# Mixer column blocks multiplied with tokens on partitions and moved through DRAM, and one half-to-half product per SSD group

## The chip, the cores and the metric

One core of one Trainium2 chip. The metric is the device time of the whole kernel in microseconds, the median of repeated runs.

## The reference

One layer of a hybrid block on 256 tokens of width 2048, all float32: a half-step SwiGLU FFN, a mixer, and a second FFN, each behind an RMS norm with adaLN modulation from a vector c. What matters here is the mixer:

```python
u = hn @ w_in                      # 2048 columns -> z, xbc, dt, q, k, v, q_idx, k_idx, w_idx, gates
xbc = silu(causal_dwconv(xbc, conv_w, conv_b))    # 4 taps along the tokens; xs, B and C
# SSD scan, per group of 4 heads (8 groups, state 128, head size 64)
y_diag = einsum('btsg,btsgr,bsgrp->btgrp', cb, decay, xc)
y_off  = einsum('btgn,bgrpn,btgr->btgrp', cc, state, exp(acum))
y = rms((y + d_skip * xs) * silu(z)) per group
y_att = top-k sparse attention(q, k, v, q_idx, k_idx, w_idx)
merged = g0 * (y_ssd @ w_br_ssd) + g1 * (y_att @ w_br_att);  out = merged @ w_out
```

## The kernel before

Every weight is used in units of 256 rows by 512 columns (512 KB). SP loads a unit into one of four slots of `raw` (L733). ScalarE rounds it to `w_hi` (L1002, `cast`), VectorE takes the rest, `w_lo` = `raw` - `w_hi` (L1536, `sub`), and TensorE multiplies it in three terms. There are four slots of `w_hi` and `w_lo`: the cast of unit n waits until unit n-4 is multiplied, and the load of unit n until unit n-4 is subtracted. So ScalarE and VectorE can be up to three units ahead of TensorE. There are 850 units in all.

The order of everything else is written out by hand. Each engine runs one loop over the unit number n; at fixed distances from a block's start or end it does the side work of that n after its own cast or subtraction (on TensorE before the unit). An engine works strictly in its order, so a wait in side work holds back the casts, subtractions or units behind it.

The mixer multiplies `w_in` in 20 column blocks of 8 units (`WBLOCKS`): b 0 and 1, c 2 and 3, xs 4 to 7, z 8 to 11, index queries qi 12 and 13, k 14, v 15, q 16 to 19. Two units of narrow front columns (step sizes, index key and weights) lie between blocks 1 and 2. Block b goes to PSUM banks 2 (b % 2) and the next; block b+2 waits for `pair_read[b % 2]`.

- Blocks of kind z, k, v, q use `unit` (L2433): tokens on partitions, 128 tokens stationary, 512 weight columns moving, 12 matmuls a unit.
- Blocks 1 to 7, 12 and 13 use `fm_unit` (L2733): 128 weight columns stationary, 256 tokens moving, 24 matmuls a unit, so that channels lie on partitions. The convolution and the index products need that layout.

After a b, c or xs block ScalarE copies the product from PSUM (`conv_in`, L1234, at n = end + 2) into `padded` and, scaled and biased, into `conv`; VectorE adds three taps, four instructions each, at end + 3, 4, 5 (`conv_tap`, L2042); ScalarE applies SiLU at end + 6. xs blocks must go back to tokens on partitions: VectorE turns them in 32x32 blocks at end + 7 (`xs_bands`, L2056), POOL stores them to DRAM, waits, and reads them back in four DMAs (L941, L910), and ScalarE spreads them at end + 13 (`xs_out`, L1275). The same trip serves the FFN activations (L1803, L916, L919, L1113) and others.

The SSD work runs by group g from `ssd_start[g]` (s): TensorE makes the B-C products at s (L2794); VectorE the segments at s + 2 (L2113); ScalarE the exponentials at s + 3: `decay_off`, four instructions for the half-to-half decay (L1364), and one for the other two; VectorE the masked decays at s + 4 (three products, `ssd_mask`, L2142); TensorE twelve products at s + 5 (`ssd_y`, L2803); VectorE the gating at s + 7 (L2153 to L2158) and the normalisation and turning at s + 9. Step sizes (`dt_first`, `dt_rest`, L2076 to L2103) are worked out at 5 and 7 to 10 units after the front columns, the cumulative sums (L2783) at block 4. The index products are one every two units from block 14 on, the top-k rounds (L2236) in the first q block, 16.

Between all this VectorE keeps adding up adaLN vectors (L1556, `ada_add`) on the units that `light` picks. Weight rows for it are loaded by SP (L739), 512 KB each.

The diff touches, beside declarations: `light`, the SP loop, the POOL loop of the mixer, `conv_in`, `qi_out`, `decay_off`, `decay_exp` and the ScalarE mixer loop, `conv_tap`, `cum_out`, `ssd_mask`, `ssd_gate` and the VectorE mixer loop, `fm_unit`, `ssd_products`, `ssd_y`, `index` and the TensorE mixer loop.

Of the kernel before, what the change touches and what calls it, by code (L numbers as in the profile page):

```python
# [23 lines left out]
F32 = mybir.dt.float32  # L24
# [6 lines left out]
P = 128  # L31
T = 256
# [88 lines left out]
def build(nc, x, c, positions, w_ada, b_ada, norm_ffn1, ffn1_w1, ffn1_w3, ffn1_w2, norm_mix, w_in,  # L121
# [50 lines left out]
    xs_raw = place("xs_raw", at_h + 4 * KB, [BANDS, UNIT // BANDS])  # L172
    kiT = place("kiT", region(T * 4), [T])
# [8 lines left out]
    acum = place("acum", region(3 * SSD_H * 4), [3, SSD_H])  # L182
# [50 lines left out]
    decay = place("decay", at_y, [3, 4, P])  # L233
    cb = place("cb", at_y + 6 * KB, [3, P])
# [36 lines left out]
    xs_dram = nc.dram_tensor("xs_bands", (P, BANDS, UNIT // BANDS), F32).ap()  # L271
    y_dram = nc.dram_tensor("y_bands", (P, BANDS, P), F32).ap()
# [79 lines left out]
    conv_out = sem("conv_out")  # L352
    xs_blocked = sem("xs_blocked")
# [19 lines left out]
    off_ready = sem("off_ready")  # L373
# [67 lines left out]
    ssd_start = [start[at_block["z"] + 1 + g] for g in range(GROUPS)]  # L441
# [286 lines left out]
    def _(sp):  # L728
# [18 lines left out]
        for f in range(2):  # L747
# [90 lines left out]
    def _(pool):  # L838
# [97 lines left out]
        for n in range(MIX, M1):  # L936
            for b in range(NW):
                if kind[b] == "xs" and n == end[b] + 7:
# [31 lines left out]
    def _(act):  # L970
# [263 lines left out]
        def conv_in(b):  # L1234

            act.wait_ge(unit_done, end[b])
# [74 lines left out]
        def qi_out(b):  # L1311
            i = WBLOCKS[b][1]
            act.wait_ge(unit_done, end[b])
            for j in range(2):
                ins = nc.scalar.activation(qiT[:, 4 * i + 2 * j:4 * i + 2 * j + 2, :],
                                           psum[:, pair(b) + j, :].rearrange("p (k t) -> p k t", k=2), ACT.Copy)
            ins.then_inc(pair_read[b % 2], 1)
# [46 lines left out]
        def decay_off(g):  # L1364
# [1688 lines left out]
```

## Time and profile before

| | |
|---|---|
| median of 3 runs | 2501.76 us (2498.63 to 2503.24) |
| profiled execution | 2502.94 us, span 2501.2 us |
| granted TensorE clock | 0.999 of full speed over the span |
| TensorE, VectorE, ScalarE, POOL busy | 99%, 75%, 47%, 7% |
| DRAM traffic | 642.76 MB, mean 257 GB/s |

The profile times single instructions of the profiled execution, in microseconds from the start of the span. The difference between span and time (1.74) lies outside the span. A matmul's duration overlaps with that of the next, so lengths of TensorE work are read from starts to starts. An idle time has behind it what ended it.

### The profile page before, as it was taken

The page shows a single profiled execution, that of the slowest core. Times are in us where ns is not written, and L with a number is a line of the kernel's source. Part 1 is how long each engine was busy: PE and PEld are TensorE (multiplying, and loading weights), DVE is VectorE, ACT ScalarE, POOL GpSimd, SP SyncE. Part 2 cuts the span into 40 slices and gives each one's busy share as a digit, 9 for nine tenths or more (in the row PEclk, how much of TensorE's full clock was granted, in tenths as well). Part 3 has the DMA queues.
Part 4 walks back from the last instruction along what each step waited for, and adds up shares of the span by engine and source line. Part 5 has one row for each costly group of instructions (what it writes and reads, how often), then busy time and mean ns, then how long its engine had stood idle before and what let it go on. Part 6 is the DMA issues. An engine that isn't in the chain of part 4 may idle for free.

```text
span 2501.2 us, 33094 instructions
## 1 busy us (share of the span) xinstructions
PE 2467.9 (99%) x12067; PEld 2080.9 (83%) x12067; DVE 1871.6 (75%) x2124; ACT 1167.4 (47%) x1431; POOL 169.9 (7%) x273
## 2 busy tenths in 40 slices
PE   7999999999999999999999999999999999999999
PEld 5788888888889999898788888888788888888887
DVE  6886679898988989988975677776789555555556
ACT  4444444444446655655555444444544444444443
POOL 4210000000000000111100000000000000000000
PEclk9999999999999999999999999999999999999999
DMA  9986679999986889985544788796698767677775
GB/s 366 376 285 191 192 246 364 311 359 304 360 289 222 274 279 317 317 251 177 177 139 139 255 278 292 255 316 242 224 318 299 224 210 210 209 210 208 211 210 173
DMA packets 290611, 642.76 MB, mean 257 GB/s; under 512 B 26066, under 2 KB 26676, under 8 KB 289588
## 3 DMA queue, kind: packets, MB, share of 16 engines
q1 hardware_dynamic: 269600, 571.41, 69.5%
q0 software_dynamic: 19136, 65.05, 7.9%
q10 hardware_dynamic: 1748, 4.62, 0.5%
q8 instruction: 78, 1.28, 0.2%
q14 instruction: 49, 0.40, 0.0%
HBM read 622.59 MB, written 18.41 MB: 256 GB/s over the span
## 4 chain that ended last, share of the span: by engine, by line
PE 91%; DVE 5%; DMA 2%; issue 1%; ACT 1%; ACTq 0%; DVEq 0%; SPq 0%
PE psum L2443 26%; PE psum L2445 26%; PE psum L2444 26%; PE psum L2743 3%; PE psum L2745 3%; PE psum L2744 3%; PE psum L2781 2%; DMA raw<-in_ffn_w 1%; DVE w_lo L1536 1%; PE psum L2431 1%; DVE ada_acc L1650 1%; DMA badas<-in_b_ada 0%; DMA gate_mix<-gate_rows 0%; PE psum L2524 0%; ACT w_hi L1002 0%
## 5 line engine op out<-in xcount | busy, mean ns | idle before, releaser
L1536 DVE TENSOR_TENSOR w_lo<-raw,w_hi 128x1024 fp32r<-128x1024 f32 (+1 forms) x850 | 1032.9, 1220 | 477.6 <-ACT w_hi L1002 475.7
L1002 ACT ACTIVATE w_hi<-raw 128x1024 fp32r<-128x1024 f32 (+1 forms) x850 | 898.2, 1059 | 1041.1 <-PE psum L2445 801.6
L2443 PE MATMUL psum<-w_hi,xT_hi 128*128 128x512 f32 x1984 | 782.3, 394 | 5.4 <-issue 3.5
L2445 PE MATMUL psum<-w_hi,xT_lo 128*128 128x512 f32 x1984 | 773.3, 390 | 0.0
L2444 PE MATMUL psum<-w_lo,xT_hi 128*128 128x512 f32 x1984 | 772.8, 390 | 0.0
L2443 PEld LDWEIGHTS psum<-w_hi,xT_hi 128*128 128x128 f32 x1984 | 372.9, 188 | 88.4 <-issue 8.7
L2445 PEld LDWEIGHTS psum<-w_hi,xT_lo 128*128 128x128 f32 x1984 | 372.7, 188 | 78.7
L2444 PEld LDWEIGHTS psum<-w_lo,xT_hi 128*128 128x128 f32 x1984 | 373.0, 188 | 76.1
L2443 PE MATMUL psum<-w_hi,aT_hi 128*128 128x512 f32 x704 | 274.8, 390 | 2.3 <-DVE aT_lo L1811 2.3
L2445 PE MATMUL psum<-w_hi,aT_lo 128*128 128x512 f32 x704 | 274.0, 389 | 0.0
L2444 PE MATMUL psum<-w_lo,aT_hi 128*128 128x512 f32 x704 | 273.9, 389 | 0.0
L1556 DVE SCALAR_TENSOR_TENSOR ada_acc<-ada_raw,cact,ada_acc 128x1024 f32<-128x1024 f32 x210 | 268.3, 1278 | 2.7 <-DMA ada_raw<-in_w_ada 2.7
L2743 PE MATMUL psum<-xT_hi,w_hi 128*128 128x256 f32 x576 | 163.6, 284 | 1.1 <-DVE w_lo L1536 1.1
L2745 PE MATMUL psum<-xT_hi,w_lo 128*128 128x256 f32 x576 | 163.0, 283 | 0.0
L2744 PE MATMUL psum<-xT_lo,w_hi 128*128 128x256 f32 x576 | 163.0, 283 | 0.0
L2443 PEld LDWEIGHTS psum<-w_hi,aT_hi 128*128 128x128 f32 x704 | 132.1, 188 | 30.5 <-issue 3.1
L2445 PEld LDWEIGHTS psum<-w_hi,aT_lo 128*128 128x128 f32 x704 | 132.1, 188 | 27.6
L2444 PEld LDWEIGHTS psum<-w_lo,aT_hi 128*128 128x128 f32 x704 | 132.2, 188 | 27.2
L1828 DVE TENSOR_TENSOR y<-psum,y 128x1024 f32<-128x1024 f32 x89 | 108.7, 1221 | 21.2 <-PE psum L2445 21.2
L2743 PEld LDWEIGHTS psum<-xT_hi,w_hi 128*128 128x128 f32 x576 | 110.5, 192 | 1.2 <-issue 1.2
L2744 PEld LDWEIGHTS psum<-xT_lo,w_hi 128*128 128x128 f32 x576 | 110.5, 192 | 0.0
L2745 PEld LDWEIGHTS psum<-xT_hi,w_lo 128*128 128x128 f32 x576 | 110.5, 192 | 0.0
(285 smaller groups left out, 2069.8 us busy)
## 6 DMA issues: line engine op xcount, KB each, us to landing
raw<-in_ffn_w SPq DMA_DIRECT2D x528, 512.0 KB, 4.6
ada_raw<-in_w_ada SPq DMA_DIRECT2D x224, 512.0 KB, 6.3
raw<-in_w_in SPq DMA_DIRECT2D x224, 512.0 KB, 4.6
ada_raw<-in_w_ada POOLq DMA_DIRECT2D x32, 512.0 KB, 6.9
ada_more<-in_w_ada POOLq DMA_DIRECT2D x32, 512.0 KB, 7.7
raw<-in_w_br_ssd SPq DMA_DIRECT2D x32, 512.0 KB, 5.3
raw<-in_w_br_att SPq DMA_DIRECT2D x32, 512.0 KB, 4.7
raw<-in_w_out SPq DMA_DIRECT2D x32, 512.0 KB, 5.2
```

The lines of the kernel that those rows point to most:

```text
L1002: nc.scalar.activation(w_hi[:, n.slot(SPLIT), 0:size], raw[:, n.slot(RAW), 0:size], ACT.Copy).then_inc(hi_ready, 1)
L1536: nc.vector.tensor_tensor(w_lo[:, n.slot(SPLIT), 0:size], raw[:, n.slot(RAW), 0:size], w_hi[:, n.slot(SPLIT), 0:size], ALU.subtract).then_ ...
L1556: nc.vector.scalar_tensor_tensor(out=acc[:], in0=src, scalar=cact[:, k:k + 1], in1=acc[:], op0=ALU.mult, op1=ALU.add).then_inc(ada_used, 1)
L1650: ins = nc.vector.scalar_tensor_tensor(out=acc[:, cols], in0=row[:, cols], scalar=cact[:, k + r:k + r + 1], in1=acc[:, cols], op0=ALU.mult ...
L1828: nc.vector.tensor_tensor(y[:, :, cols], psum[:, bank:bank + HALF, :], y[:, :, cols], ALU.add).then_inc(y_added, 1)
L2443: nc.tensor.matmul(o, hi[:, kt + k, toks], whi, start=a, stop=False)
L2444: nc.tensor.matmul(o, hi[:, kt + k, toks], wlo, start=False, stop=False)
L2445: ins = nc.tensor.matmul(o, lo[:, kt + k, toks], whi, start=False, stop=b)
L2743: nc.tensor.matmul(o, w_hi[:, s, cols], xT_hi[:, kt + k, :], start=a, stop=False, skip_group_check=True)
L2744: nc.tensor.matmul(o, w_hi[:, s, cols], xT_lo[:, kt + k, :], start=False, stop=False, skip_group_check=True)
L2745: ins = nc.tensor.matmul(o, w_lo[:, s, cols], xT_hi[:, kt + k, :], start=False, stop=b, skip_group_check=True)
L2781: return nc.tensor.matmul(o, a, b, start=first, stop=last)
```

## The change

Blocks 1 to 7, 12 and 13 are multiplied with `unit` as the others, and `fm_unit` is gone. At end + 2 VectorE turns the product from PSUM in 32x32 blocks into `mix_blk` (two instructions of 512 columns, new `product_bands`); POOL stores it to DRAM (512 KB), waits for the store, and reads it back in four DMAs of 128 KB into `mix_raw`. ScalarE reads that at end + 8 (`READ_AT`), in `conv_in` or `qi_out`, instead of PSUM at end + 2. The taps follow at +1, +2, +3, SiLU at +4, the turning of xs at +5 and `xs_out` at +11 from there; block 0 keeps its places. `ssd_start` moves four units later for every group, and `light` keeps adaLN adds off other units. There is one `mix_blk` and one `mix_raw`.

Per group, the half-to-half part no longer has a decay matrix: the decay is split into a factor per source token (with the step size, `acum[:, 2]`) and one per target token (`acum[:, 3]`), exponentiated once for all groups (`far_decay`, `far_weights`). VectorE scales xs by the first (`x_far`), TensorE multiplies once with the B-C product, 256 columns, into bank 4, and VectorE scales the result by the second (`y_far`) and adds it.

The core of the diff:

```diff
+    BANDED = [b for b in range(1, NW) if kind[b] in ("b", "c", "xs", "qi")]
+    READ_AT = 8
+    conv_at = [end[b] + (READ_AT if b else 2) for b in range(at_block["z"])]
-    ssd_start = [start[at_block["z"] + 1 + g] for g in range(GROUPS)]
+    ssd_start = [start[at_block["z"] + 1 + g] + UPB // 2 for g in range(GROUPS)]
...
-        return w % UPB not in (3, 4, 5) if w < 9 * UPB else w == 9 * UPB + 1 or w % UPB in (0, 3, 5, 6)
+        return w % UPB not in (1, 2, 3) if w < 10 * UPB else w % UPB in (1, 2, 4, 7)
...
                         if g >= 2:
-                            sp.wait_ge(off_ready, g - 1)
...
+                if b in BANDED and n == end[b] + 2:
+                    i = BANDED.index(b)
+                    pool.wait_ge(pair_read[b % 2], b // 2 + 1)
+                    if i:
+                        pool.wait_ge(mix_read, i)
+                    pool.dma_start(mix_dram, mix_blk[:]).then_inc(mix_stored, 16)
+                    pool.wait_ge(mix_stored, 16 * (i + 1))
+                    bands_to(mix_raw, mix_dram, mix_moved)
...
+                act.wait_ge(mix_moved, 16 * BANDS * (BANDED.index(b) + 1))
...
-            for j in range(2):
-                src = psum[:, pair(b) + j, :].rearrange("p (k t) -> p k t", k=2)
-                nc.scalar.activation(padded[:, b % 2, 2 * j:2 * j + 2, 3:3 + T], src, ACT.Copy)
+            for half in range(HALF):
+                dst = padded[:, b % 2, :, 3 + half * P:3 + (half + 1) * P].rearrange("p k (b t) -> p k b t", t=32)
+                nc.scalar.activation(dst, by_bands(half, mix_raw), ACT.Copy)
...
-                ins = nc.scalar.activation(conv[:, k, :], psum[:, pair(b) + k // 2, (k % 2) * T:(k % 2 + 1) * T],
+                ins = nc.scalar.activation(y_tokens(conv, k), mix_bands(k),
...
-            ins.then_inc(pair_read[b % 2], 1)
+            ins.then_inc(mix_read, 1)
...
-            for k in range(4):
-                ins = nc.scalar.activation(decay[:, 1, k, :], cum_spread[:, g % 2, k, P:T], ACT.Exp,
-                                           bias=acum[:, 2, 4 * g + k:4 * g + k + 1])
-            ins.then_inc(off_ready, 1)
+        def far_decay():
+
             act.wait_ge(acum_ready, 1)
+            nc.scalar.activation(acum[:, 2:4, :], acum[:, 2:4, :], ACT.Exp).then_inc(far_exp, 1)
...
                 if n == CUM_AT + 2:
                     cum_copy()
+                    far_decay()
...
+        def product_bands(b):
+
+            i = BANDED.index(b)
+            dve.wait_ge(unit_done, end[b])
+            dve.wait_ge(h_spilled, 16)
+            if i:
+                dve.wait_ge(mix_stored, 16 * i)
+            for half in range(HALF):
+                ins = nc.vector.transpose(mix_blk[:].rearrange("p c (k s t) -> p s k c t", s=HALF, t=32)[:, half],
+                                          psum[:, pair(b) + half, :].rearrange("p (k c t) -> p k c t", c=BANDS, t=32))
+            ins.then_inc(pair_read[b % 2], 1)
...
+            dve.wait_ge(far_ready, 1)
+            nc.vector.tensor_tensor(x_far[:], heads4(xs[:, g])[:, 0], head_cols(2, g), ALU.mult)
-            for j in range(3):
+            for j in (0, 2):
...
+            nc.vector.tensor_tensor(y_far[:], psum[:, 4, 0:T].rearrange("p (k d) -> p k d", k=4), head_cols(3, g),
+                                    ALU.mult).then_inc(y_step, 1)
...
+            nc.vector.tensor_tensor(yg2[:, 1, :], yg2[:, 1, :], y_far[:].rearrange("p k d -> p (k d)"), ALU.add).then_inc(y_step, 1)
...
+                pe.wait_ge(y_step, 4 * g - 2)
...
-                o = psum[:, 7, T + k * 64:T + (k + 1) * 64]
-                plain(o, decay[:, 1, k, :], xdt[:, 0, k, :], True, False)
-                ins = plain(o, decay[:, 2, k, :], xdt[:, 1, k, :], False, True)
-            ins.then_inc(y_raw, 1)
+                plain(psum[:, 7, T + k * 64:T + (k + 1) * 64], decay[:, 2, k, :], xdt[:, 1, k, :])
+            plain(psum[:, 4, 0:T], cb[:, 1, :], x_far[:].rearrange("p k d -> p (k d)")).then_inc(y_raw, 1)
...
-                if kind[b] in ("b", "c", "xs", "qi"):
-                    fm_unit(n, 2 * u, 2 * (b % 2), u == 0, u == UPB - 1)
-                else:
-                    unit(At(n), xT_hi, xT_lo, 2 * u, 2 * (b % 2), u == 0, u == UPB - 1)
+                unit(At(n), xT_hi, xT_lo, 2 * u, 2 * (b % 2), u == 0, u == UPB - 1)
```

## Rows read from the trace of the kernel before

**Rows 1.** The page: busy time, and the chain that ended last.
```profile
PE 2467.9 (99%) x12067; PEld 2080.9 (83%) x12067; DVE 1871.6 (75%) x2124; ACT 1167.4 (47%) x1431; POOL 169.9 (7%) x273
...
PE 91%; DVE 5%; DMA 2%; issue 1%; ACT 1%; ACTq 0%; DVEq 0%; SPq 0%
```

**Rows 2.** The chain in order of time: start, length, what.
```profile
887.21 1.26 PE psum L2781 x10
...
980.70 0.23 PE psum L2443
...
1002.49 0.65 PE psum L2781 x4
...
1016.77 2.62 PE psum L2781 x24
...
1242.64 0.86 PE psum L2781 x4
```

**Rows 3.** ScalarE's timeline at block 6: start, length, line, what, idle before.
```profile
934.66 1.09 ACT L1257 ACTIVATE padded<-psum 128x512 f32<-128x512 f32 x2 [1.76 <-PE psum L2745]
...
937.42 2.03 ACT L1002 ACTIVATE w_hi<-raw 128x1024 fp32r<-128x1024 f32 x2
```

**Rows 4.** VectorE's timeline at the same place.
```profile
938.54 1.22 DVE L1536 TENSOR_TENSOR w_lo<-raw,w_hi 128x1024 fp32r<-128x1024 f32 x1 [2.12 <-ACT w_hi L1002]
939.68 1.67 DVE L2052 SCALAR_TENSOR_TENSOR conv<-padded,convT,conv 128x256 f32<-128x256 f32 x4
941.27 1.22 DVE L1536 TENSOR_TENSOR w_lo<-raw,w_hi 128x1024 fp32r<-128x1024 f32 x1
```

**Rows 5.** Busy time by stretch: the top-k rounds.
```profile
1188.00:1230.00 42.00, 40.27 (x193) 32.84 (x191) 41.45 (x105) 21.34 (x32) 9.53 (x14) 1.00 0.53 152
```

**Rows 6.** Timelines of VectorE, POOL and ScalarE: three trips through DRAM.
```profile
951.53 1.30 DVE L2064 STREAM_TRANSPOSE xs_blk<-conv 128x512 f32<-128x512 f32 x2
953.13 0.56 POOL L941 DMA_DIRECT2D xs_bands<-xs_blk  x1 [16.92 <-DVE xs_blk L2064]
958.12 2.18 POOL L910 DMA_DIRECT2D xs_raw<-xs_bands  x4 [4.43 <-DMA xs_bands<-xs_blk]
968.10 1.34 ACT L1283 ACTIVATE xs<-xs_raw 128x256 f32<-128x256 f32 x4 [3.52 <-DMA xs_raw<-xs_bands]
...
975.10 1.30 DVE L2064 STREAM_TRANSPOSE xs_blk<-conv 128x512 f32<-128x512 f32 x2
...
992.43 1.34 ACT L1283 ACTIVATE xs<-xs_raw 128x256 f32<-128x256 f32 x4 [5.10 <-DMA xs_raw<-xs_bands]
...
1842.93 1.31 DVE L1803 STREAM_TRANSPOSE act_blk<-act_tok 128x512 f32<-128x512 f32 x2
...
1857.96 1.15 ACT L1113 ACTIVATE aT_hi<-aT_raw 128x512 fp32r<-128x512 f32 x2 [2.33 <-DMA aT_raw<-act_bands]
```

**Rows 7.** ScalarE's timeline at the front columns.
```profile
853.43 0.20 ACT L1301 ACTIVATE wi<-psum 128x32 f32<-128x32 f32 x1 [0.79 <-DVE sp_e L2080]
...
853.99 1.28 ACT L1305 ACT_TABLE_LOAD   x1
...
855.45 1.99 ACT L1002 ACTIVATE w_hi<-raw 128x1024 fp32r<-128x1024 f32 x2
```

**Rows 8.** VectorE's timeline at the step-size series.
```profile
857.66 1.28 DVE L1556 SCALAR_TENSOR_TENSOR ada_acc<-ada_raw,cact,ada_acc 128x1024 f32<-128x1024 f32 x1
858.86 0.19 DVE L2087 TENSOR_SCALAR sp_s<-sp_e 128x64 f32<-128x64 f32 x1
...
860.41 1.23 DVE L1536 TENSOR_TENSOR w_lo<-raw,w_hi 128x1024 fp32r<-128x1024 f32 x1
...
862.75 0.74 DVE L2093 SCALAR_TENSOR_TENSOR sp_p<-sp_p,sp_e 128x64 f32<-128x64 f32 x3
```

**Rows 9.** Busy time of block 7 (last two columns: DMA share, GB/s); DMA traffic of 10 to 60 us.
```profile
957.00:980.70 23.70, 23.70 (x199) 23.70 (x198) 21.32 (x28) 13.23 (x19) 2.74 (x5) 1.00 1.00 337
...
DMA packets 6778, 18.92 MB, mean 378 GB/s; under 512 B 665, under 2 KB 993, under 8 KB 6777
```

More of the change, by code:

```diff
@@ L937, in _ @@
             for b in range(NW):
-                if kind[b] == "xs" and n == end[b] + 7:
+                if b in BANDED and n == end[b] + 2:
[6 more added lines that the diff above has]
+                    bands_to(mix_raw, mix_dram, mix_moved)
+                if kind[b] == "xs" and n == conv_at[b] + 5:
                     i = WBLOCKS[b][1]
@@ L1234, in conv_in @@
         def conv_in(b):
-            act.wait_ge(unit_done, end[b])
+            if b == 0:
+                act.wait_ge(unit_done, end[b])
+            else:
+                act.wait_ge(mix_moved, 16 * BANDS * (BANDED.index(b) + 1))
             act.wait_ge(pads, 1)
@@ L1312, in qi_out @@
             i = WBLOCKS[b][1]
[L1313 to L1317, printed above, removed]
+            act.wait_ge(mix_moved, 16 * BANDS * (BANDED.index(b) + 1))
+            for half in range(HALF):
+                ins = nc.scalar.activation(by_tokens(qiT[:, 4 * i:4 * i + 4, :], half), by_bands(half, mix_raw), ACT.Copy)
+            ins.then_inc(mix_read, 1)
         def v_out(b):
@@ L1440, in mixer @@
                     if kind[b] in ("b", "c", "xs"):
-                        if n == end[b] + 2:
+                        if n == conv_at[b]:
                             conv_in(b)
-                        if n == end[b] + 6:
+                        if n == conv_at[b] + 4:
                             conv_silu(b)
-                        if kind[b] == "xs" and n == end[b] + 13:
+                        if kind[b] == "xs" and n == conv_at[b] + 11:
                             xs_out(b)
+                    if kind[b] == "qi" and n == end[b] + READ_AT:
+                        qi_out(b)
                     if n == end[b] + 2:
@@ L2044, in conv_tap @@
             if j == 0:
-                dve.wait_ge(pair_read[b % 2], b // 2 + 1)
+                dve.wait_ge(mix_read, BANDED.index(b) + 1) if b else dve.wait_ge(pair_read[0], 1)
                 dve.wait_ge(pads, 1)
@@ L2054, in conv_tap @@
                                                op0=ALU.mult, op1=ALU.add).then_inc(taps, 1)
+        def product_bands(b):
[4 more added lines that the diff above has]
+                dve.wait_ge(mix_stored, 16 * i)
+            for half in range(HALF):
+                ins = nc.vector.transpose(mix_blk[:].rearrange("p c (k s t) -> p s k c t", s=HALF, t=32)[:, half],
+                                          psum[:, pair(b) + half, :].rearrange("p (k c t) -> p k c t", c=BANDS, t=32))
+            ins.then_inc(pair_read[b % 2], 1)
         def xs_bands(b):
@@ L2324, in mixer @@
                 for b in range(NW):
-                    if kind[b] in ("b", "c", "xs") and n in (end[b] + 3, end[b] + 4, end[b] + 5):
-                        conv_tap(b, n - end[b] - 3)
-                    if kind[b] == "xs" and n == end[b] + 7:
+                    if b in BANDED and n == end[b] + 2:
+                        product_bands(b)
+                for b in range(NW):
+                    if kind[b] in ("b", "c", "xs") and n - conv_at[b] in (1, 2, 3):
+                        conv_tap(b, n - conv_at[b] - 1)
+                    if kind[b] == "xs" and n == conv_at[b] + 5:
                         xs_bands(b)
@@ L2731, in ffn @@
                         turn_gate((2, 8)[f], GATE_BANK[2 * f])
-        def fm_unit(n, kt, bank, first, last):
-            pe.wait_ge(split_ready, n + 1)
-            s = n % SPLIT
-            for j in range(4):
-                o = psum[:, bank + j // 2, (j % 2) * T:(j % 2 + 1) * T]
-                for k in range(2):
-                    cols = slice(k * NB + j * P, k * NB + (j + 1) * P)
-                    a, b = first and k == 0 and j % 2 == 0, last and k == 1
-                    nc.tensor.matmul(o, w_hi[:, s, cols], xT_hi[:, kt + k, :], start=a, stop=False, skip_group_check=True)
-                    nc.tensor.matmul(o, w_hi[:, s, cols], xT_lo[:, kt + k, :], start=False, stop=False, skip_group_check=True)
-                    ins = nc.tensor.matmul(o, w_lo[:, s, cols], xT_hi[:, kt + k, :], start=False, stop=b, skip_group_check=True)
-            ins.then_inc(unit_done, 1)
         def plain_unit(n, kt, first, last):
```

41 lines of the change are left out of this document (26 added, 15 removed).

## The prediction

> **What bounds the kernel now.** I read the page first: TensorE is busy 99% of the span and carries 91% of the chain that ended last [rows 1]. So a shorter TensorE stream is worth its own length wherever VectorE, ScalarE and the DMAs keep up, and the question is the mixer, where VectorE is 9 tenths busy. Then I read the chain in order of time [rows 2]. From 888.47 (887.21 and the 1.26 of the cumulative sums) to 980.70 run four column blocks in the old form, 23.06 us each, or 2.88 us a unit of 24 matmuls. From 980.70 to 1002.49 runs a block in the form that the change spreads to all: 21.79 us, 2.72 us a unit of 12 matmuls. The twelve products of a group take 2.62 us. Both stretches have no hole: TensorE bounds them.
>
> **What hides the rest today** is a lead. ScalarE may cast a unit once the unit four places ahead of it is done, so VectorE runs up to three units ahead of TensorE. I read the VectorE and ScalarE timelines for what consumes that lead. Today the copy of a finished block waits only for TensorE: it starts at 934.66, the next cast at 937.42 [rows 3], the next subtraction at 938.54 [rows 4]. Everything in the sum below is made of such steps.
>
> **The change part by part.**
>
> *Matmuls.* Nine blocks of eight units, each unit 2.88 to 2.72: 0.16 x 72 = 11.3 us less TensorE work. In block 1 (the second "b" block) VectorE already sets the pace, so only some 0.4 of its 1.3 can show.
>
> *Group products.* Twelve products at 2.62/12 = 0.22 become eight (1.75) and one of 256 columns; two such take 0.86 [rows 2], so 0.43. 2.62 to 2.18, 0.44 x 8 = 3.5 us less.
>
> *The removed exponentials* (four on ScalarE per group) are not on the path, since ScalarE is half idle (busy 47% [rows 1]): nothing. *VectorE per group:* one decay product less, two 256-wide and one PSUM product more: about +0.4 us beside 24.7 us of TensorE work: nothing either. *The last-but-one stretch*, from 1188, where VectorE has the top-k rounds and works 41.45 of 42 us [rows 5]: groups move four units later, so one gate and one normalisation leave the rounds and land behind them. I add the same durations up both ways and get TensorE about 0.7 us earlier. *SP:* no DMA more; one wait less. *POOL:* per block one store, a wait and four reads, 0.56 + 2.18 us of issuing [rows 6], in a queue that is otherwise waiting.
>
> *The round trip.* This decides. The product of a block is turned at unit 2 after its end, and is read by ScalarE at unit 8. Rows of the same trip (512 KB out, four reads of 128 KB, same queue) give the time from the first transpose to ScalarE's start when ScalarE sat waiting for it: 951.53 to 968.10 = 16.6, 975.10 to 992.43 = 17.3, 1842.93 to 1857.96 = 15.0 [rows 6]. The trace doesn't show this trip beside a second one. I take the mean, 16.3, for blocks 1 to 4 and the largest, 17.3, for blocks 5 to 7, where the old xs trip shares the DMA queues; the ends for the range are 15.0, and 19 as an estimate (17.3 and a tenth more, for the larger traffic).
>
> *The loop.* ScalarE can't cast unit 1 of the next block until it has read the trip (2.76 [rows 3]; strided reads from SBUF, I take the same). VectorE then subtracts, runs four taps, subtracts, and only then turns the next block: 1.14 + 1.59 + 1.14 = 3.9 [rows 4]. So from one turning to the next: trip 16.3 + copy 2.8 + cast 1.1 + 3.9 = 24.1 us, against 21.8 us of TensorE. No lead survives a loop that is 2.3 us too long per block. Today it doesn't exist: the copy hangs on TensorE alone.
>
> Step by step, time 0 being the end of block 1, and "ready" the end of a unit's subtraction, which is 16.3 + 5.0 after a turning:
> - Trip 1 starts at 0.3. ScalarE reads it at unit 6 of block 2, and there also does the front columns, 853.43 to 855.45 = 2.0 [rows 7]. Unit 7 is ready at 23.6; TensorE wants it at 24.9 (5.8 for two front units, seven of 2.72).
> - Now the taps of block 1 fall on the units in which the step-size series is worked out (1.55, then 0.7 to 1.1 [rows 8]) and an adaLN add (1.2 [rows 8]) is kept. The next four units are ready 5.5, 4.7, 3.5 and 3.5 later: 40.8 for unit 3 of block 3, wanted at 35.8. Stall 5.0.
> - Trip 2 (37.3) makes unit 1 of block 4 ready at 58.6; TensorE is there at 58.4.
> - In block 4 the new exponential of the far weights waits on ScalarE for VectorE's unit 2, which now holds turning, taps and copies (1.2 + 1.6 + 0.5), then loads a table (1.28 [rows 7]) and exponentiates (0.3); the cast of unit 3 is queued behind, and its subtraction: 68.4 instead of 64.0. Stall 4.4, and 0.6 for the table that goes back. Trip 3 (61.3) hides in it.
> - Trip 4 (86.5): unit 1 of block 6 at 107.8. Trips 5, 6, 7, with 17.3, are loops of 25.0: 132.8, 157.8, 182.8.
>
> Before, the same stretch (to unit 1 of block 9) is 5.8 + 6 x 23.06 + 21.8 + 2.7 + 1.3 + 0.2 for two small transposes = 170.2. So this stretch gets **12.6 us longer**, though its TensorE work is 7.6 us shorter.
>
> Behind it the DMAs are lighter, the groups' TensorE work grows to 24.7 per block, and the lead comes back; the two index blocks turn their products with no taps behind: 2 x 1.3 gained, 3.5 from the groups, 0.7 from the top-k stretch, and 0.7 lost in block 9, which starts with no lead.
>
> Sum: +12.6 - 0.4 - 2.6 - 3.5 - 0.7 + 0.7 = **+6.1 us**. The profiled execution took 2502.94 (span 2501.2), 1.2 above the median of 2501.76. Against the median the forecast is 2508, slower by 0.25%; 0.2% (5 us) is about what a measurement of this kernel can tell from no change.
>
> *DMA traffic.* A block with the old xs trip moves 8.0 MB today (23.7 us at 337 GB/s, share 1.00), and one with both trips 9.0: over the 25.0 us of the loop 360 GB/s. The trace has held 378 GB/s for 50 us [rows 9], so I give it no stall of its own. The Trainium skill (DMA: Bandwidth & Descriptors, Specifications) puts the limit of HBM at about 358 GB/s for a core. By that rule 9.0 MB would need an estimated 25.1 us, which leaves the sum with the loop where it is and would take some 8 us from a version without it; the trace, at 378, disagrees.
>
> **The rivals.**
> 1. *The lead holds, and the kernel is faster.* If the trips are short enough, the loop fits under a block of TensorE work and every stall but those of blocks 3 and 4 goes. For it: today an xs trip blocks ScalarE for up to 5.1 us per block and TensorE never stops. Against it: that trip is followed by a copy which hangs on TensorE, so its lateness isn't handed on. It decides from a trip of 14.0 us down (21.8 - 2.8 - 1.1 - 3.9), shorter than any row shows. Worth -11.3 - 3.5 - 0.7 with 0.9 lost in block 1, about 2 in the clashes of blocks 3 and 4, 1 elsewhere: -11.6, 2490.
> 2. *Short trips.* The loop as I say but all trips at 15.0: 1.3 less for the first trip, 1.3 + 3 x 2.3 for the last four: -9.5 on my sum, -3.4, so 2498.
> 3. *The DMAs bind.* The raw loads and the two trips share one set of queues, and casts wait for weights. At the 337 GB/s of today's fullest block [rows 9] 9.0 MB take 26.7 us, 1.7 more than my loop in blocks 6 and 7 and half of that in block 8, and the longer xs trip then delays unit 4 as well, about 1 in each: +7.3 on the sum, 2515. It decides from about 360 GB/s down, the rate that my loop itself asks for.
> 4. *The new form isn't shorter here.* It stands in the same stage at 2.72 a unit [rows 2], so this has almost no chance.
>
> **How the numbers follow.** My case 0.47 (its own range 2502 to 2513; about two thirds of its chance lie above 2506.8), rival 1 0.18, rival 2 0.18, rival 3 0.15, rival 4 0.02. Slower by over 0.2% (above 2506.8): 0.31 + 0.15 = 0.46. Faster by over 0.2% (below 2496.8): 0.18 and a quarter of rival 2, together 0.22. Within: what is left, 0.32. The range reaches from just above rival 1 to just above rival 3: 2491 to 2516.
>
> **What would show it.** In the changed profile: units of the nine blocks at 2.72 and group products at 2.18; TensorE idle until VectorE's subtraction in blocks 3 to 8, 15 to 20 us in all, and nearly none before; ScalarE waiting for the trip in each of them and VectorE for ScalarE's cast; turnings 24 to 25 us apart; one idle of some 4 us in block 4, behind the far exponential. I am wrong if the turnings are 21.8 apart with TensorE solid (rival 1), or if casts wait for weights rather than for the trip (rival 3).

## The result: 2520.3 us, slower by 0.75%

The changed kernel took 2520.3 us in the median of 4 runs (2516.1 to 2522.6), the kernel before 2501.75 (2498.6 to 2503.2) beside it: ratio 1.0075, 95% interval 1.0063 to 1.0087. I forecast 2508 and a range to 2516. The sign was right, the size was a third of what came.

The profile after, first the page's lines that answer to [rows 1]:

```profile
span 2520.9 us, 31318 instructions
PE 2466.6 (98%) x11155; PEld 2034.4 (81%) x11155; DVE 1886.5 (75%) x2160; ACT 1161.0 (46%) x1402; POOL 194.8 (8%) x318
...
PE 82%; DVE 7%; DMA 6%; ACT 2%; issue 2%; POOL 0%; ACTq 0%; DVEq 0%; SPq 0%
```

TensorE has the shorter stream, and its share of the chain fell from 91% to 82%; the DMAs' rose from 2% to 6%. The chain in order of time shows one turn of what took its place (start, length, what):

```profile
871.87 1.32 DVE mix_blk L2082 x2
...
873.47 5.03 DMA mix_bands<-mix_blk
...
878.78 1.63 POOL mix_raw L925 x3
880.41 8.59 DMA mix_raw<-mix_bands
...
890.09 2.06 ACT conv L1286 x4
892.15 0.96 ACT w_hi L1025
...
894.27 1.66 DVE conv L2070 x4
895.94 1.14 DVE w_lo L1554
897.07 1.23 DVE mix_blk L2082 x2
```

From turning to turning, no TensorE in it: VectorE turns, the bands go to DRAM and come back, ScalarE reads them and only then casts, VectorE subtracts, runs taps, subtracts and turns the next block. I call this chain, which ends where it begins, the ring. ScalarE's timeline has the waits for the trips, at the end of each:

```profile
850.99 1.16 ACT L1283 ACTIVATE padded<-mix_raw 128x512 f32<-128x512 f32 x2 [4.28 <-DMA mix_raw<-mix_bands]
889.03 1.15 ACT L1283 ACTIVATE padded<-mix_raw 128x512 f32<-128x512 f32 x2 [2.97 <-DMA mix_raw<-mix_bands]
912.93 1.16 ACT L1283 ACTIVATE padded<-mix_raw 128x512 f32<-128x512 f32 x2 [0.30 <-DMA mix_raw<-mix_bands]
938.84 1.16 ACT L1283 ACTIVATE padded<-mix_raw 128x512 f32<-128x512 f32 x2
964.78 1.16 ACT L1283 ACTIVATE padded<-mix_raw 128x512 f32<-128x512 f32 x2 [4.81 <-DMA mix_raw<-mix_bands]
991.43 1.16 ACT L1283 ACTIVATE padded<-mix_raw 128x512 f32<-128x512 f32 x2 [3.73 <-DMA mix_raw<-mix_bands]
1018.53 1.16 ACT L1283 ACTIVATE padded<-mix_raw 128x512 f32<-128x512 f32 x2 [3.72 <-DMA mix_raw<-mix_bands]
```

VectorE in turn waits for ScalarE's cast, and TensorE for VectorE's subtraction. The two engines behind the reading at 964.78:

```profile
968.89 1.22 DVE L1554 TENSOR_TENSOR w_lo<-raw,w_hi 128x1024 fp32r<-128x1024 f32 x1 [3.65 <-ACT w_hi L1025]
970.03 1.67 DVE L2070 SCALAR_TENSOR_TENSOR conv<-padded,convT,conv 128x256 f32<-128x256 f32 x4
971.61 1.22 DVE L1554 TENSOR_TENSOR w_lo<-raw,w_hi 128x1024 fp32r<-128x1024 f32 x1
972.75 1.30 DVE L2082 STREAM_TRANSPOSE mix_blk<-psum 128x512 f32<-128x512 f32 x2
...
970.16 0.50 PE L2494 MATMUL psum<-w_hi,xT_hi 128*128 128x512 f32 x1 [2.25 <-DVE w_lo L1554]
```

The turnings (VectorE, L2082) stand at 833.46, 871.87, 896.99, 920.91, 946.81, 972.75 and 999.39. So from the second on the trips take 17.2, 15.9, 17.9, 18.0, 18.7 and 19.1, the turnings come 25.1, 23.9, 25.9, 25.9 and 26.6 apart, and each period is its trip and 8.0 us. Between 800 and 1300 us TensorE shows 18 idles of over 0.5 us, some 30 us together (before: 3, 3.1 us). Idles are counted here and below from start to start, less the usual distance of two matmuls; the timeline's own idle times are up to 0.2 us shorter.

A reading that I had not looked for stands behind the longer idles. Granted clock (after the busy times of PE, PEld, DVE, ACT, POOL) in two windows of ten microseconds:

```profile
core 0: us, PE busy (x) PEld busy (x) DVE busy (x) ACT busy (x) POOL busy (x), PEclk, DMA share, GB/s
900.00:910.00 10.00, 7.33 (x25) 5.78 (x25) 8.71 (x13) 7.45 (x8) 2.18 (x4) 0.83 0.84 256
1020.00:1030.00 10.00, 7.26 (x20) 5.43 (x19) 7.37 (x13) 7.74 (x14) 2.18 (x4) 0.66 0.82 254
```

In the second, TensorE idles for 2.9 us from 1021.0, and the next 13 matmuls stand 0.43 us apart instead of 0.23: the lower of its two levels, 1.2 GHz for 2.4. Between 800 and 1300 us three such stretches follow idles (8, 13 and 7 matmuls, 5.6 us more than at full clock); in the kernel before there is none there.

**Where the time went**, by TensorE's timeline. Up to the end of block 1 the two executions differ by 3.4 us in favour of the changed kernel, of which at most 0.4 can be its units in block 1: the rest is the same program, and executions of one kernel vary by as much. From there to unit 1 of block 9 the kernel before took 834.92 to 1005.73, 170.8 us; the changed one 831.56 to 1023.91, 192.3: 21.5 us more. The next 13 matmuls run at half clock, 2.6 more. Up to the last index product (block 15) 6.6 come back, behind it 5.4 go: 2.2 of these are only the products of one group, which now stand behind that point instead of ahead of it, and 3.2 are lost, where the top-k rounds are. Together 22.9, less 3.4: the 19.5 by which the spans differ (19.7). The medians differ by 18.6.

### The profile page after: what moved, and what is told of

Read it like the earlier page. It is cut to its first block, busy times and chain, and to the rows that moved or that the text cites. A ratio compares the mean times of both kernels' runs of the same rounds, so it can differ in the third digit from the quotient of the medians.

```text
span 2520.9 us, 31318 instructions
## 1 busy us (share of the span) xinstructions
PE 2466.6 (98%) x11155; PEld 2034.4 (81%) x11155; DVE 1886.5 (75%) x2160; ACT 1161.0 (46%) x1402; POOL 194.8 (8%) x318
## 4 chain that ended last, share of the span: by engine, by line
PE 82%; DVE 7%; DMA 6%; ACT 2%; issue 2%; POOL 0%; ACTq 0%; DVEq 0%; SPq 0%
PE psum L2494 26%; PE psum L2496 26%; PE psum L2495 26%; DVE w_lo L1554 2%; PE psum L2817 2%; DMA mix_raw<-mix_bands 2%; DMA raw<-in_ffn_w 2%; DMA mix_bands<-mix_blk 1%; PE psum L2482 1%; DVE conv L2070 1%; ACT w_hi L1025 1%; DVE ada_acc L1668 1%; ACT conv L1286 0%; POOL mix_raw L925 0%; DVE mix_blk L2082 0%
## 5 line engine op out<-in xcount | busy, mean ns | idle before, releaser
L2494 PE MATMUL psum<-w_hi,xT_hi 128*128 128x512 f32 x2272 | 900.8, 396 | 32.1 <-DVE w_lo L1554 29.2
L2495 PE MATMUL psum<-w_lo,xT_hi 128*128 128x512 f32 x2272 | 888.4, 391 | 0.0
L2496 PE MATMUL psum<-w_hi,xT_lo 128*128 128x512 f32 x2272 | 888.0, 391 | 0.0
L2494 PEld LDWEIGHTS psum<-w_hi,xT_hi 128*128 128x128 f32 x2272 | 428.7, 189 | 136.2 <-DVE w_lo L1554 32.1
L2496 PEld LDWEIGHTS psum<-w_hi,xT_lo 128*128 128x128 f32 x2272 | 428.6, 189 | 91.0
L2495 PEld LDWEIGHTS psum<-w_lo,xT_hi 128*128 128x128 f32 x2272 | 428.7, 189 | 87.0
L2494 PE MATMUL psum<-w_hi,yT_hi 128*128 128x512 f32 x128 | 50.6, 395 | 0.0
L2494 PE MATMUL psum<-w_hi,mT_hi 128*128 128x512 f32 x128 | 50.5, 395 | 0.0
L2496 PE MATMUL psum<-w_hi,mT_lo 128*128 128x512 f32 x128 | 50.0, 390 | 0.0
L2496 PE MATMUL psum<-w_hi,yT_lo 128*128 128x512 f32 x128 | 49.9, 390 | 0.0
```

Source lines behind the costliest of these rows:

```text
L2494: nc.tensor.matmul(o, hi[:, kt + k, toks], whi, start=a, stop=False)
L2495: nc.tensor.matmul(o, hi[:, kt + k, toks], wlo, start=False, stop=False)
L2496: ins = nc.tensor.matmul(o, lo[:, kt + k, toks], whi, start=False, stop=b)
```

## The experiments

All ratios are to the kernel before on the same chip, with their 95% intervals.

**1. The ring opened: the reading later.**

```
 READ_AT = 8
+CONV_READ = 10
-conv_at = [end[b] + (READ_AT if b else 2) ...]
+conv_at = [end[b] + (CONV_READ if b else 2) ...]
-return w % UPB not in (1, 2, 3) if w < 10 * UPB ...
+return w % UPB not in (3, 4, 5) if w < 10 * UPB ...
...
```

The second edit moves the adaLN adds off the units that now hold the taps. The first SSD group also waits for the last taps and the last turning of xs, which come later.

> The changed kernel with one schedule number moved: ScalarE reads the mixer trips of the tap blocks at unit 10 after a block's end instead of 8, so the taps, the cumulative-sum copies excepted, come two units later, and ScalarE's reading no longer stands ahead of the cast that VectorE needs before the next turning. Loop theory (trip, then copy, cast, four taps and the next turning in a ring): the ring is open, turnings come 21.8 to 22.9 us apart in blocks 4 to 9, about 15 us of TensorE's 21 lost in blocks 3 to 9 come back, together with the stretches at half clock: about 2505 us (2500 to 2511), ratio to before 1.001. The old xs trip has a ring of its own (trip 16.6, copy 2.9, cast 1.1, two subtractions 2.3 = 22.9), which may keep some 3 us of that. Rival, the DMAs bind: the same bytes in the same blocks, so turnings stay 25 to 26 us apart and the time at 2517 to 2522.

Measured: 2506.2 us, ratio 1.0029 (1.0020 to 1.0039), 11.5 us less than the changed kernel by the two ratios. ScalarE never waits for the mixer trip any more. The ring was the largest part of the loss, as the first theory said. Its size was not as I had said. The 2505 looks met, but the kernel before took 2499.7 beside this run, so the ratio is 1.0029 and not 1.001: 11.5 us came back, not 15. The turnings are 24.7, 22.2, 24.0, 23.1 and 25.9 apart, not 21.8 to 22.9, and TensorE keeps 11 idles of over 0.5 us, 17.0 us together. That is for experiments 6 to 8.

Here, too, three of the five periods are turning to reading plus a fixed rest, 2.5 us, which is VectorE's subtraction and add between a cast and the turning. So a fixed rest alone doesn't show a ring. What does are the waits for the trip, which are gone here, and the time that their end gives back.

**2. Fewer bytes beside the ring, and fewer bytes in it.** The first leaves out the xs trip, 1 MB for each of four blocks:

```
-act.wait_ge(xs_moved, 16 * BANDS * (i + 1))
+act.wait_ge(xs_blocked, i + 1)
...
-src = xs_raw[:] ...
+src = xs_blk[:] ...
...
-pool.dma_start(xs_dram, xs_blk[:]).then_inc(xs_stored, 16)
-pool.wait_ge(xs_stored, 16 * (i + 1))
-bands_to(xs_raw, xs_dram, xs_moved)
...
```

> The changed kernel without the old xs trip through DRAM (ScalarE copies from the transposed tile in SBUF, so the xs values stand in the wrong order): 1 MB less for each of four blocks, and ScalarE never waits for it. The mixer ring is untouched. Theory that the traffic of the second trip lengthens the first one: the trips of blocks 5 to 8 fall from 17.9-19.1 to about 16.3 us, the turnings from 25.9-26.7 to about 24.1 apart, total about 2512 us. Rival, a trip takes its 18 us whatever runs beside it: turnings stay above 25.5 apart, total 2517 to 2520.

Measured: 1.0075 (1.0061 to 1.0089), no change at all; turnings 24.2, 22.7, 26.5, 25.3 and 26.1 apart, the last three trips 17.3, 18.1 and 17.6 long (18.0, 18.7 and 19.1 in the changed kernel). My theory that the second trip lengthens the first by some 2 us fell. The last three are 0.6 to 1.5 us shorter here, but trips at the same place differ from trace to trace, too: in experiment 4, where no byte is left out, the same three took 17.9, 17.9 and 18.6. So little of a trip can be the xs trip's doing. The second has the mixer trips carry half of their bytes:

```
-pool.dma_start(mix_dram, mix_blk[:]).then_inc(mix_stored, 16)
+pool.dma_start(mix_dram[0:64], mix_blk[0:64]).then_inc(mix_stored, 16)
...
-bands_to(mix_raw, mix_dram, mix_moved)
+for to in range(BANDS):
+    pool.dma_start(mix_raw[32 * to:32 * (to + 1), 0:2], mix_dram[0:64, to, :]...)
...
```

> The changed kernel, the mixer trips with half of their bytes: two of the four token bands go to DRAM (256 KB) and come back (four reads of 64 KB), the rest of the tile is zero, so half of each turned product is missing; waits, queues and the number of instructions stay. The bytes taken away (0.5 MB written and 0.5 MB read for a block) are as many as dropping the xs trip takes, which moved neither the time nor the turnings. Ring theory: trips of 12 to 14 us, the ring of 20 to 22 us fits under TensorE's 21.8, turnings 22 to 23 apart from block 4 on: about 2509 us (2506 to 2512). Rival, the bytes on the shared queues matter and not where they are in the ring: as without the xs trip, 2518.

Measured: 1.0022 (1.0013 to 1.0031), 13 us less than the changed kernel. The turning of block 3, ScalarE's reading of it and the next turning, from its two timelines:

```profile
917.26 1.30 DVE L2088 STREAM_TRANSPOSE mix_blk<-psum 128x512 f32<-128x512 f32 x2
...
933.60 1.16 ACT L1289 ACTIVATE padded<-mix_raw 128x512 f32<-128x512 f32 x2 [1.85 <-DMA mix_raw<-mix_bands]
...
941.57 1.31 DVE L2088 STREAM_TRANSPOSE mix_blk<-psum 128x512 f32<-128x512 f32 x2
```

Trip 16.3, period 24.3, difference 8.0. Over its five periods the trips are 14.8, 13.9, 16.3, 15.3 and 15.6, the periods 22.7, 22.2, 24.3, 23.2 and 23.6: again trip + 8.0 in each (8.2 once). In two of the five (13.9 and 15.6) ScalarE came from a cast that had waited for its weights and no longer for the trip, so there the trip is no longer what sets the period. The trips shrank less than I said (12 to 14), since half of the bytes is not half of the time.

The two runs take about the same out of the DRAM traffic of the whole kernel, 4.2 MB without the xs trip and 4.7 MB here. (For one block the expectation counts double: the half trip saves 0.25 MB written and 0.25 MB read, against 0.5 and 0.5 for the xs trip.) At the one place none of the loss comes back, at the other 13 us: the trip's place in the ring is shown.

**3. Is VectorE's load the brake of the changed kernel?** In the adaLN adds of blocks 4 to 9 only 4 columns are added:

```
+few = 32 <= mixed[0] - FRONT_END + 2 * UPB < 80
-ada_add(At(e * KT + k), k)
+ada_add(At(e * KT + k), k, slice(0, 4) if few else slice(0, ADA_COLS))
```

> The changed kernel, the adaLN adds of blocks 4 to 9 on 4 columns instead of 1024 (so most of these sums is left out; their loads stay). VectorE does some 27 adds of 1.2 us less there. Ring theory: no add stands in the ring (trip, copy, cast, subtraction, taps, subtraction, turning), so the turnings stay trip + 8.0 us apart, 25 to 26.5, and the time at 2516 to 2520. Rival, VectorE's load (22.5 us of work in a block of an xs column) is what stops TensorE: turnings 22 to 23 apart, about 2506.

Measured: 1.0082 (1.0068 to 1.0096), periods 24.8, 23.0, 26.0, 25.3 and 26.9 with trips of 16.8, 15.0, 18.0, 17.3 and 18.9: trip + 8.0 once more. VectorE works 22 us less (22 adds shortened by 1 us each, not the 27 that I had counted on), and it gives nothing, because none of it stands in the ring.

**4. The far exponential in block 4.**

```
 if n == CUM_AT + 2:
     cum_copy()
-    far_decay()
+if n == CUM_AT + 6:
+    far_decay()
...
-if n == CUM_AT + 3:
+if n == CUM_AT + 7:
     far_weights()
```

> The changed kernel with the far weights' exponential (and VectorE's product behind it) four units later. In the trace it costs 2.8 us of idle and a stretch at half clock in block 4. By the steps of my prediction that stall hid the ring's own, and taking it away gives 2.7 us: 2517.5. By the ring as measured (trip 17 + 8.0 = 25 from the turning at 897.1, the next one stands at 921.0 already) nothing is left to give back: 2519 to 2521. Rival, the whole of idle and half clock comes back: 4 us, 2516.

Measured: 2518.2 us, 1.0073 (1.0059 to 1.0087). The difference to the changed kernel, 0.5 us, lies inside both intervals, and between the three numbers that I had written down this one can't choose with certainty; it is nearest to the ring's (0). The periods in the trace do: 25.0 and 23.8 around block 4, against 25.1 and 23.9 with the exponential in its place. The same move in the kernel of experiment 1:

> The kernel with the late reading, and the exponential of the far weights four units later in block 4. In the changed kernel it stood in front of a cast and cost a 2.8 us idle and a stretch at half clock; with the late reading block 4 shows no idle above 0.5 us, since the taps no longer share its unit. Expected: nothing, 2505 to 2507. Rival, it still delays a cast and the lead: 2 us less, 2504.

Measured: 1.0027 (1.0016 to 1.0038) against 1.0029: nothing, as expected.

**5. The group part alone, and its start four units later.** To the kernel before, first only the far weights, the one product per group and VectorE's two added operations, with `ssd_start` and the places of the adds as they were:

> The kernel before with the group part of the change alone (one half-to-half product per group, far weights, two more VectorE operations), at its old place, no block turned. By my sum: 0.44 us of TensorE less in each of eight groups, no stall: about 2498 us, ratio 0.9986. Rival, the far exponential and VectorE's extra work eat it: 2501 to 2503.

Measured: 2498.3 us, 0.9990 (0.9981 to 0.9999), 2.5 us less; I had 3.5. Then with the changed kernel's start and its places for the adaLN adds:

```
-ssd_start = [start[at_block["z"] + 1 + g] for g in range(GROUPS)]
+ssd_start = [start[at_block["z"] + 1 + g] + UPB // 2 for g in range(GROUPS)]
...
-return w % UPB not in (3, 4, 5) if w < 9 * UPB else w == 9 * UPB + 1 or w % UPB in (0, 3, 5, 6)
+return w % UPB not in (3, 4, 5) if w < 10 * UPB else w % UPB in (1, 2, 4, 7)
```

> As the kernel with the group part alone, and the groups started four units later with the changed kernel's places for the adaLN adds. By my sum another 0.7 us less than the group part alone: ratio 0.9983. Rival, the shift is what made the top-k stretch 5 us longer in the changed kernel (VectorE's queue, then a stretch of half clock): 4 to 5 us more than the group part alone, ratio about 1.0004.

Measured: 1.0001 (0.9992 to 1.0010). The two together cost about 2.8 us, where my sum had a gain of 0.7; what the adds' places cost alone was not run. VectorE's timeline at the end of the top-k rounds shows where it goes:

```profile
1220.93 1.21 DVE L1531 TENSOR_TENSOR w_lo<-raw,w_hi 128x1024 fp32r<-128x1024 f32 x1
1222.06 0.69 DVE L2160 TENSOR_TENSOR yg<-xs,skip 128x512 f32<-128x512 f32 x1
1222.66 0.42 DVE L2162 TENSOR_TENSOR y_far<-psum,acum 128x256 f32<-128x256 f32 x1
1222.99 0.68 DVE L2165 TENSOR_TENSOR yg<-psum,yg 128x512 f32<-128x512 f32 x1
1223.71 0.43 DVE L2167 TENSOR_TENSOR yg<-yg,y_far 128x256 f32<-128x256 f32 x1
1224.17 0.69 DVE L2169 TENSOR_TENSOR yg<-yg,zs 128x512 f32<-128x512 f32 x1
1224.78 0.42 DVE L2259 TENSOR_SCALAR score<-score 128x512 f32<-128x512 f32 x1
1225.12 0.69 DVE L2260 SCALAR_TENSOR_TENSOR dist<-banned,dist 128x512 f32<-128x512 f32 x1
1225.84 0.69 DVE L2262 TENSOR_TENSOR dist<-dist,score 128x512 f32<-128x512 f32 x1
1226.45 1.22 DVE L1531 TENSOR_TENSOR w_lo<-raw,w_hi 128x1024 fp32r<-128x1024 f32 x1
```

The gate of the last group does leave the rounds, but lands in the unit behind them, in one piece with the mask's last steps: 5.5 us from one subtraction to the next, with no adaLN add among them, where TensorE needs 2.7. There was no lead left from the rounds, so TensorE idles (its timeline follows with experiment 9). In the changed kernel the same pair of idles stands at 1229.3 (1.3 us) and 1248.4 (2.6), with 1.4 of half clock behind: 5.3 us, where the kernel before idles for 1.9.

**6 to 8. What holds the blocks of the xs columns once the ring is open?** The kernel of experiment 1 with the edit of experiment 2 (no xs trip), then with that of experiment 3 (short adds), then with both:

> The kernel with the late reading and without the xs trip through DRAM (the xs values again in the wrong order). There the ring is open, but casts wait for the weights for up to 5 us at a time, and blocks 6 to 9 still lose about 10 us of TensorE at a DMA share of 1.00 to 1.05. Theory, once the ring is open the DMAs bind there: 1 MB less for each of four blocks gives 5 to 8 us, about 2499. Rival, these stalls are the xs trip's own ring (ScalarE waits 4.5 to 4.8 us for it): then they go too, but the casts' waits for weights stay as long as they are. Third, neither: 2506.

Measured: 1.0016 (1.0007 to 1.0025), 3 us less than experiment 1 by the ratios, though the intervals overlap; the casts still wait for weights, so it is the third case with a small gain.

> The kernel with the late reading and the same short adds. There the ring is open, and turnings are 23.1 to 25.9 apart in blocks 5 to 9. Theory, what is left there is VectorE's own work, 22.5 us a block against TensorE's 21.8, plus its waits for casts: without the adds it has 5 to 6 us less a block, turnings 21.8 to 22.2, the 7 us of idle in blocks 5 to 9 go: about 2499. Rival, the casts' waits for weights on full DMA queues (share 1.00 to 1.05): the bytes are the same, so turnings stay 23 to 25 apart and the time at 2503 to 2506.

Measured: 1.0040 (1.0026 to 1.0054), if anything more than experiment 1. Periods 23.8, 23.1, 23.0, 24.9 and 26.3. VectorE's load alone is not what holds these blocks: in its window of 50 us it works 34 of 50, and TensorE still idles.

```profile
core 0: us, PE busy (x) PEld busy (x) DVE busy (x) ACT busy (x) POOL busy (x), PEclk, DMA share, GB/s
950.00:1000.00 50.00, 44.67 (x191) 34.97 (x190) 34.16 (x57) 25.61 (x38) 10.02 (x19) 1.00 1.04 341
```

> The kernel with the late reading, without the xs trip and with the short adds, both at once (xs values in the wrong order, most of the adaLN sums of blocks 4 to 9 left out). Each alone gave next to nothing. Theory, two limits stand side by side there: VectorE's 22.5 us of work a block once the queues are lighter, and queues that deliver the weights of a block in 23 to 24 us once VectorE is lighter. Taking both away: turnings 21.8 to 22.5 apart in blocks 5 to 9, their idle of about 6 us gone, 2498 to 2501. Rival, a third thing holds these blocks (the loads of the mixer trip and the adaLN rows alone fill the queues): as each alone, 2505 to 2508.

Measured: 1.0007 (0.9998 to 1.0016), some 5.5 us less than experiment 1: more than either alone, less than the theory of two limits wanted (2498 to 2501; it came to 2502.5). Periods 23.3, 23.1, 22.7, 23.8 and 24.2, and blocks 5 to 9 keep 4.4 us of idles, five of 0.7 to 1.0 us. ScalarE's timeline before one of them (TensorE's at 963.5), in experiment 8:

```profile
954.51 1.06 ACT L1020 ACTIVATE w_hi<-raw 128x1024 fp32r<-128x1024 f32 x1 [2.75 <-DMA raw<-in_w_in]
957.14 1.06 ACT L1020 ACTIVATE w_hi<-raw 128x1024 fp32r<-128x1024 f32 x1 [1.57 <-DMA raw<-in_w_in]
958.11 1.14 ACT L1278 ACTIVATE padded<-mix_raw 128x512 f32<-128x512 f32 x2
959.15 2.06 ACT L1281 ACTIVATE conv<-mix_raw,vecT,convT 128x256 f32<-128x256 f32 x4
961.12 2.94 ACT L1020 ACTIVATE w_hi<-raw 128x1024 fp32r<-128x1024 f32 x3
```

Three casts stand ready behind the 3 us in which ScalarE reads the trip, and the two before it had come late, with their weights. So here the reading costs TensorE a microsecond, as the weights have left no lead. That the other four come about in the same way is likely, not shown. Why the weights come late even with 1 MB less was not settled; the mixer trip's own bytes and the four raw buffers were not varied.

**9. Idle and clock.** Twelve matmuls that nothing reads, in front of the wait that ends the idle of experiment 5:

```
+if n == start[at_block["q"]] + 12:
+    pe.wait_ge(rel_ready, 8)
+    for i in range(12):
+        plain(psum[:, 6, :], xT_hi[:, 0, 0:P], xT_hi[:, 2:4, :])
```

> The group part with the shifted start (its TensorE idles for 2.7 us at about 1225 until VectorE's subtraction, and the next 7 matmuls come 0.43 apart instead of 0.23), with 12 matmuls of 512 columns that nothing reads put in front of that wait: TensorE multiplies through most of the idle. If the half clock follows from the idle: no matmul at 0.43 behind it, 1.4 us back at that place, and up to 0.3 lost where the filling is longer than the idle; in total within 0.1% of the group part with the shifted start. If the clock falls for another reason: the stretch at 0.43 stays.

TensorE's timeline without them:

```profile
1224.82 0.39 PE L2458 MATMUL psum<-w_hi,xT_lo 128*128 128x512 f32 x1
1227.72 0.50 PE L2456 MATMUL psum<-w_hi,xT_hi 128*128 128x512 f32 x1 [2.51 <-DVE w_lo L1531]
...
1228.75 0.54 PE L2457 MATMUL psum<-w_lo,xT_hi 128*128 128x512 f32 x1
1229.09 0.63 PE L2458 MATMUL psum<-w_hi,xT_lo 128*128 128x512 f32 x1
1229.51 0.63 PE L2456 MATMUL psum<-w_hi,xT_hi 128*128 128x512 f32 x1
1229.94 0.63 PE L2457 MATMUL psum<-w_lo,xT_hi 128*128 128x512 f32 x1
```

and with them:

```profile
1222.36 2.88 PE L2794 MATMUL psum<-xT_hi 128*128 128x512 f32 x12
1225.08 0.44 PE L2456 MATMUL psum<-w_hi,xT_hi 128*128 128x512 f32 x1
...
1227.18 0.39 PE L2456 MATMUL psum<-w_hi,xT_hi 128*128 128x512 f32 x1
1227.41 0.39 PE L2457 MATMUL psum<-w_lo,xT_hi 128*128 128x512 f32 x1
```

No matmul at 0.43 is left. In time the two are alike, 1.0001 (0.9992 to 1.0010), as 1.4 us must be.

That the filling kept the clock up is not shown by this. The same wait, unfilled, stands in eleven traces here with an idle of 2.6 to 2.7 us. Eight have a stretch at half clock behind it and three have none (experiments 1, 4 and 8). Experiment 8's, TensorE's timeline:

```profile
1226.79 0.50 PE L2494 MATMUL psum<-w_hi,xT_hi 128*128 128x512 f32 x1 [2.51 <-DVE w_lo L1549]
1227.13 0.39 PE L2495 MATMUL psum<-w_lo,xT_hi 128*128 128x512 f32 x1
```

The profiled execution of experiment 8 was granted full clock up to its last microsecond, behind idles of up to 3.4 us too, and so was the one with the filling. In the changed kernel four idles of over 2 us (2.2, 2.7, 2.4 and 2.6) have no half clock behind them, in the run without the xs trip one of 2.2 has. What can be said is the other way round: between 800 and 1300 us every stretch at half clock in the sixteen traces stands behind an idle of 2.2 us or more.

**10 and 11. What can be kept.** The kernel before with the group part of experiment 5 and only the two index blocks turned:

```
+BANDED = [b for b in range(1, NW) if kind[b] == "qi"]
...
-if kind[b] in ("b", "c", "xs", "qi"):
+if kind[b] in ("b", "c", "xs"):
     fm_unit(n, 2 * u, 2 * (b % 2), u == 0, u == UPB - 1)
```

> The kernel before with the group part (at its old place) and only the two index blocks turned (tokens on partitions, trip, read eight units later), the seven tap blocks left in the old form. No taps follow there, and the DMAs are at 0.6 to 0.8. By my sum: 2 x 1.3 us on top of the group part, ratio 0.998, about 2495.5. Rival, the index products or the top-k stretch take it back: as the group part alone, 0.999.

Measured: 2495.7 us, ratio 0.9982 (0.9973 to 0.9991): faster than both kernels, by 4.5 and some 23 us. It idles nowhere that the group part alone did not. And a version with three tap blocks turned as well, no block with two trips:

```
+conv_at = [end[b] + {"b": 12 if b else 2, "c": 10, "xs": 6}[kind[b]] for b in range(at_block["z"])]
...
+return w in (19, 20, 21) or w % UPB not in (3, 4, 5) if w < 46 else w % UPB not in (7, 0, 1) if w < 74 ...
```

> A version meant to keep what pays: group part at its old place, the two index blocks and three of the seven tap blocks (the second b block and both c blocks) turned, read 12, 10 and 10 units after their end so that no ring closes; the four xs blocks stay in the old form, read at 6 instead of 2, so that no block has two trips. By the sum: 3 x 1.3 us less than with the index blocks alone, 1 to 2 lost in the clash of taps and adds: ratio to before 0.997, about 2493. Rival, the late places of the xs taps cost VectorE its lead: 0.998 to 1.000.

Measured: 0.9991 (0.9982 to 1.0000), so the rival. TensorE runs through blocks 4 to 8 without an idle, but the first three blocks have four, 5.8 us (experiment 10: one, 1.2), 4.6 more, against the 3.9 us that the shorter units bring.

## Why the prediction was too low

**Right: the mechanism.** Trip, copy, cast, taps and turning in a ring that is longer than TensorE's block, no lead surviving it, idles until VectorE's subtraction in blocks 3 to 9. I had the constant at 7.8 (2.8 + 1.1 + 3.9); it is 8.0. Right too: the units at 2.72 and a group's products at 2.22 (I said 2.72 and 2.18); the stretch before at 170.8 (170.2; I had left out the first group's B-C products, 0.6); and what comes back behind it, 6.6 - 2.2 = 4.4 us, or 5.0 with these products, which now stand in it, against 2.6 + 3.5 - 0.7 = 5.4. The chance of slower, 0.46, was the largest of the three.

**Failed first: the length of the trips.** "I take the mean, 16.3, for blocks 1 to 4 and the largest, 17.3, for blocks 5 to 7." From the first turning, they took 17.5, 17.2, 15.9, 17.9, 18.0, 18.7 and 19.1. The term for the whole stretch was +12.6, and the trace says +21.5. By its places, counted from the end of block 1:

- The first turning comes at 1.9, not 0.3, and its trip is 1.2 longer: the second turning stands at 40.3 instead of 37.3, 3.0 late.
- The next five periods sum to 127.5 instead of 123.3 (37.3 to 61.3 to 86.5, then 24.1 and twice 25.0): 4.2 more.
- The last trip is 1.8 longer, and 0.5 goes in what follows it. That makes 192.3 instead of 182.8, 9.5 more; the stretch before is itself 0.6 longer than I had summed it, so the term is 8.9 too small.

Of the 9.5, the seven trips make 7.2, and the first turning, which VectorE reaches later than I had placed it, 1.6.

The upper end that I had kept, 19, is what the last trip has. I put it into no rival and hardly into the range, and a term that seven trips multiply needs that most of all. The reason that I gave for the longer trips in the later blocks, the xs trip on the same queues, isn't the main one: without it the last three were 17.3 to 18.1 (experiment 2). The rows of before show a trip beside the raw and adaLN loads alone; which of the bytes lengthens it was not separated.

**Failed next: the top-k stretch.** "I add the same durations up both ways and get TensorE about 0.7 us earlier." The sum of durations was the wrong view. What counts is the subtraction that comes late, and the moved gate sits in the unit with the mask's last steps. The changed kernel lost 3.2 us there, 3.9 off my term; the shift with the adds' new places, on a kernel that still has its lead, costs 2.8.

**Not in the sum: the clock.** I priced an idle at its length. Behind three of the idles stood matmuls at 0.43 us instead of 0.23, 5.6 us in all. Inside the ring that cost nothing more, as TensorE was not the bound there; behind it, at 1024.5 and 1248.9, 2.6 and 1.4 us were on the path.

**The stall of block 4** (4.4 us in my steps) exists in the trace as an idle of 2.8 us and 8 slow matmuls, yet is worth nothing, or 0.5 us: the ring's own period fills the same time. I had said that trip 3 hides in it and had 2.7 us to spare; with trips at 17 there is nothing to spare.

**Rival 1, the lead holds,** would hardly have come even with short trips. Opening the ring brought 1.0029 and not its 2490: with the ring open, casts in the xs blocks wait for weights, up to 5.6 us at a time. That is the mechanism of rival 3, which I let decide only between rates of 337 and 360 GB/s. In the changed kernel its place is small (casts waited for weights there too, but ScalarE waited longer for the trip).

**DMA rates.** I weighed a page of the Trainium skill (DMA: Bandwidth & Descriptors, Specifications), which gives about 358 GB/s as a core's limit, against 378 GB/s over 50 us in the trace [rows 9]. The 25-us windows of experiment 1 moved 358 and 347 GB/s at shares of 1.04 and 1.05, with casts waiting for weights. By that rule these windows stand at the limit; the trace of before went beyond it with other traffic (large loads, no trips). Whether the small trips among the loads make the difference, no run here isolates. I also wrote that the raw loads and the trips share one set of queues. The page lists SP's loads on q1 and POOL's trips on q0; what they share are the 16 DMA engines, whose busy share these windows give.

## What to carry to other kernels

When a hand-over between engines is made longer, look for the first later instruction, on the engine that waits for it, that the next hand-over needs: if there is one, the trip is in a ring. Once the trip and everything between are longer than the block, their sum is the period, whatever TensorE does. Such a ring multiplies the error of its longest term by its turns, so the range has to carry the worst row of that term, not the mean; and reading two steps later, without a byte less, opens it. Sums of work over a stretch say little of an engine without a lead: place each moved operation in its unit and look for the fullest one.

## What was unexpected of the hardware

- Between 800 and 1300 us the sixteen traces have 44 idles of TensorE of 2.2 to 3.6 us. Behind 27 of them, at once or after up to six matmuls at full clock, 5 to 13 matmuls came 0.43 us apart, half clock; behind the 12 idles of 1.6 to 2.1 us none did. An idle of TensorE cost up to 2.6 us more than its length. Which idles are followed by it differs from execution to execution at the same place.
- A trip of 512 KB out and back took 15.9 to 19.1 us, half of the bytes 13.9 to 16.3. Over the same five trips the mean fell from 17.5 to 15.2, so by an estimate from these two means some 5 of the 17.5 us go with the bytes, and the larger part doesn't.
- Taking 1 MB a block from DMA engines at a share of 1.0 changed nothing while the ring closed, and 3 us of 2506 once it was open (intervals overlapping).
